# Sparse attention's scores from queries and keys split into a high and a low part

## What is computed

```python
q = _rope(q.reshape(B_, S_, G, Hg, Dh).transpose(0, 2, 3, 1, 4), pos)      # G=2 groups, Hg=4 heads, Dh=64
k_cmp = _rope(_compress(kv(kc), pe[0], w1[0], w2[0]), cmp_end)             # 31 compressed keys per group
s = jnp.einsum('bgjtd,bgcd->bgjtc', q, k_cmp) * scale                      # compressed scores
p_cmp = _masked_softmax(s, cmp_end[None, :] <= pos[:, None])
k_slc = _rope(kv(ks), pos)                                                 # keys of the selected blocks
sc = jnp.einsum('bgjqd,bgqnld->bgjqnl', qi, kg) * scale                    # their scores
# window branch: the same with kw, vw; the three outputs are mixed by gates
```

## Time and profile before

| | |
|---|---|
| median of 3 runs | 2645.97 us |
| lowest and highest | 2643.62 and 2646.96 us |
| the profiled execution's own time | 2646.77 us |
| its span in the profile | 2645.5 us |
| PE busy | 2613.4 us, 99% |
| DVE busy | 1563.1 us, 59% |
| ACT busy | 1037.1 us, 39% |
| mean granted clock of PE | 0.997 |

### The profile page before, as it was taken

One profiled execution on the slowest core, in us unless ns is written; L12 is line 12 of the kernel. 1 busy time (PEld: TensorE's weight loads), 2 busy tenths in 40 slices (PEclk: granted clock), 3 DMA queues, 4 the chain that ended last, 5 costly groups with the idle time before them and its releaser, 6 DMA issues.

```text
span 2645.5 us, 33775 instructions
## 1 busy us (share of the span) xinstructions
PE 2613.4 (99%) x13925; PEld 2149.9 (81%) x13925; DVE 1563.1 (59%) x2805; ACT 1037.1 (39%) x1809; POOL 15.0 (1%) x43
## 2 busy tenths in 40 slices
PE   7999999999999999999999999999999999999999
PEld 5788888898888897767888889888888766888888
DVE  7766554458666366777766637653356687633334
ACT  4652343444222245664322224222234665422223
POOL 1000000000000000000000000000000000000000
PEclk9999999999999999999999999999999999999999
DMA  8255433225555234311655424633333511233222
GB/s 260 80 175 171 131 116 112 80 84 199 195 191 175 88 113 130 110 33 49 209 200 191 163 84 156 209 125 96 96 96 110 155 33 33 85 106 96 96 92 68
DMA packets 298241, 330.14 MB, mean 125 GB/s; under 512 B 13410, under 2 KB 248678, under 8 KB 298088
## 3 DMA queue, kind: packets, MB, share of 16 engines
q1 hardware_dynamic: 297716, 327.44, 38.8%
q10 hardware_dynamic: 372, 0.55, 0.1%
HBM read 319.56 MB, written 2.10 MB: 122 GB/s over the span
## 4 chain that ended last, share of the span: by engine, by line
PE 93%; DVE 5%; ACT 1%; DMA 0%; SPq 0%; issue 0%; DVEq 0%
PE bank L543 27%; PE bank L545 27%; PE bank L544 27%; PE bank L597 2%; PE bank L2536 1%; PE bank L2563 1%; PE bank L2176 1%; DVE w_lo L511 1%; DVE E L2658 1%; PE bank L571 0%; DMA mw<-in_w_mod 0%; PE bank L573 0%; PE bank L572 0%; PE bank L900 0%; PE bank L2351 0%; PE bank L587 0%
## 5 line engine op out<-in xcount | busy, mean ns | idle before, releaser
L543 PE MATMUL bank<-h_lo,w_hi 128*128 128x512 f32 (+1 forms) x2496 | 936.1, 375 | 2.6 <-DVE h_lo L742 1.5
L545 PE MATMUL bank<-h_hi,w_lo 128*128 128x512 f32 (+1 forms) x2496 | 918.5, 368 | 0.0
L544 PE MATMUL bank<-h_hi,w_hi 128*128 128x512 f32 (+1 forms) x2496 | 917.3, 368 | 0.0
L511 DVE TENSOR_TENSOR w_lo<-raw,w_hi 128x1024 fp32r<-128x1024 f32 (+1 forms) x420 | 489.1, 1200 | 373.3 <-ACT w_hi L505 373.1
L505 ACT ACTIVATE w_hi<-raw 128x1024 fp32r<-128x1024 f32 (+1 forms) x420 | 420.1, 1036 | 349.7 <-PE bank L545 335.3
L543 PEld LDWEIGHTS bank<-h_lo,w_hi 128*128 128x128 f32 x2496 | 471.0, 189 | 88.2 <-issue 7.2
L544 PEld LDWEIGHTS bank<-h_hi,w_hi 128*128 128x128 f32 x2496 | 471.2, 189 | 78.6 <-issue 4.1
L545 PEld LDWEIGHTS bank<-h_hi,w_lo 128*128 128x128 f32 x2496 | 470.2, 188 | 78.7
L543 PE MATMUL bank<-a_lo,w_hi 128*128 128x512 f32 (+1 forms) x1056 | 388.6, 368 | 0.0
L545 PE MATMUL bank<-a_hi,w_lo 128*128 128x512 f32 (+1 forms) x1056 | 384.0, 364 | 0.0
L544 PE MATMUL bank<-a_hi,w_hi 128*128 128x512 f32 (+1 forms) x1056 | 383.9, 364 | 0.0
(11 more groups left out here) (344 smaller groups left out, 2291.3 us busy)
## 6 DMA issues: line engine op xcount, KB each, us to landing
swf<-in_w_ada SPq DMA_DIRECT2D x60, 1024.0 KB, 7.6
raw<-in_ffn_w_gate SPq DMA_DIRECT2D x44, 1024.0 KB, 5.3
raw<-in_ffn_w_up SPq DMA_DIRECT2D x44, 1024.0 KB, 5.3
raw<-in_w_in SPq DMA_DIRECT2D x40, 1024.0 KB, 5.2
raw<-in_ffn_w_down SPq DMA_DIRECT2D x32, 1024.0 KB, 5.3
raw<-in_w_in SPq DMA_DIRECT2D x32, 512.0 KB, 5.3
raw<-in_ffn_w_down SPq DMA_DIRECT2D x16, 768.0 KB, 4.4
mw<-in_w_mod SPq DMA_DIRECT2D x8, 1024.0 KB, 12.0
```

The lines of the kernel that those rows point to most:

```text
L511: nc.vector.tensor_tensor(o, r, half(w_his[place_of[i]], i, h)[0].bitcast(F32), ALU.subtract).then_inc(*w_lo.up((i, h)))
L543: nc.tensor.matmul(o, w1, al, start=start, stop=False)
L544: nc.tensor.matmul(o, w1, ah, start=False, stop=False)
L545: return nc.tensor.matmul(o, w2, ah, start=False, stop=stop)
```

## The change

Operands of the sparse scores are split into a high part (rounded to fp32r) and a low part (the rest).

- Queries: tile qa holds head 0's high part on the lower 64 partitions and its low part on the upper 64; tile qb holds head 1's low part below and its high part above. Keys: ksh and kwh hold the high parts on all 128 rows, once per half; kl the low parts.
- A score step becomes two fp32r products on 128 rows (high over low queries, with high keys), then two fp32r products on 64 rows (high queries with low keys), accumulated in the same banks. Low times low is left out.
- The compressed scores become, for each of 4 pairs c and 2 heads, one product with kc_hi (32 columns) and one with kc_lo (32 columns): 16 per call instead of 4 in fp32.
- For p = 4 to 9 ACT writes the high part in two copies of 64 x 512 (act_high) and DVE the low part in two subtractions of 64 x 512 (dve_low_part). DVE's sum of the rotary embedding now stays in its temporary tile, and ("rd", l, p) is now the low part's.
- The compressed keys get one sum on DVE, one copy on ACT (act_kc_high), two subtractions on DVE (dve_kc_low), which stand behind dve_w(("vv", l), 2).
- sp_cross copies high parts (waiting for ACT) and then waits for tile 9's low part; sp_cross_low copies the low parts, waiting for the last value product of the differential attention.
- The third output's copies move from step 28 to 32 (OC_STEP), since its place in a_hi now holds low keys until the last score.

```diff
+    def act_high(l, p):
+        act.wait_ge(dve, ("rx", l, p))
+        for par in range(2):
+            nc.scalar.activation(high_of(p, par), pair(p)[1][par * 64:par * 64 + 64, :], ACT.Copy).then_inc(
+                *act.up(("rh", l, p) if par else ("rh", l, p, 0)))
+
+    def dve_low_part(l, p):
+        dve.wait_ge(act, ("rh", l, p))
+        for par in range(2):
+            r = slice(par * 64, par * 64 + 64)
+            if p < 8:
+                o = qab[par][64 - par * 64:128 - par * 64, (p - 4) * 512:(p - 4) * 512 + 512]
+            else:
+                o = kl[p - 8][0][r, :]
+            nc.vector.tensor_tensor(o, pair(p)[1][r, :], high_of(p, par).bitcast(F32), ALU.subtract).then_inc(
+                *dve.up(("rd", l, p) if par else ("rd", l, p, 0)))
...
@@ def dve_kc
-        dve.wait_ge(pool, ("zn", l))
-        for par in range(2):
-            r = slice(par * 64, par * 64 + 64)
-            nc.vector.tensor_tensor(kcz[r, par * 64:par * 64 + 64], lamt[r, 64:128], lamt[r, 128:192], ALU.add).then_inc(
-                *dve.up(("kc", l, par)))
+        nc.vector.tensor_tensor(kb, kb, kc, ALU.add).then_inc(*dve.up(("kc", l, 0)))
+
+    def act_kc_high(l):
+        act.wait_ge(dve, ("kc", l, 0))
+        nc.scalar.activation(kc_hi, lamt[:, 64:128], ACT.Copy).then_inc(*act.up(("kch", l)))
+
+    def dve_kc_low(l):
+        dve.wait_ge(act, ("kch", l))
+        dve.wait_ge(pool, ("zn", l))
+        for par in range(2):
+            r = slice(par * 64, par * 64 + 64)
+            nc.vector.tensor_tensor(kc_lo[r, par * 64:par * 64 + 64], lamt[r, 64:128], kc_hi[r, :].bitcast(F32),
+                                    ALU.subtract).then_inc(*dve.up(("kc", l, 1 + par)))
@@ def pe_cs
-        pe.wait_ge(dve, ("kc", l, 1))
+        pe.wait_ge(dve, ("kc", l, 2))
         for c in range(4):
-            kz = kcz[:, :].rearrange("p (a g c) -> p a g c", a=2, g=2)[:, :, c // 2, :]
-            m = nc.tensor.matmul(t[:, c * 64:c * 64 + 64].rearrange("p (a c) -> p a c", a=2),
-                                 nq[:, c * 512 + b * 128:c * 512 + b * 128 + 128], kz, start=True, stop=True)
+            g = c // 2 * 32
+            for par in range(2):
+                o = t[:, c * 64 + par * 32:c * 64 + par * 32 + 32]
+                q = qab[par][:, c * 512 + b * 128:c * 512 + b * 128 + 128]
+                nc.tensor.matmul(o, q, kc_hi[:, g:g + 32], start=True, stop=False)
+                m = nc.tensor.matmul(o, q, kc_lo[:, par * 64 + g:par * 64 + g + 32], start=False, stop=True)
@@ def scores
+            pe.wait_ge(cross_low_in[br], l)
             t = [bank(("ns", l, s, par), N_SC) for par in range(2)]
+            q = [qab[par][:, c * 512 + b * 128:c * 512 + b * 128 + 128] for par in range(2)]
+            for par in range(2):
+                nc.tensor.matmul(t[par][:, 0:w], q[par], kh[br][:, g * 512:g * 512 + w], start=True, stop=False)
             for par in range(2):
                 r = slice(par * 64, par * 64 + 64)
-                k0 = (g ^ par) * 512
-                nc.tensor.matmul(t[par][:, 0:w], nq[r, c * 512 + b * 128:c * 512 + b * 128 + 128],
-                                 (ks, kw)[br][r, k0:k0 + w], start=True, stop=True).then_inc(
-                                     *pe.up(("ns", l, s, par)))
+                nc.tensor.matmul(t[par][:, 0:w], q[par][r, :], kl[br][g ^ par][r, 0:w], start=False, stop=True).then_inc(
+                    *pe.up(("ns", l, s, par)))
@@ def act_mixer
         for i in range(2):
             steps(1)
+            if i:
+                act_high(l, 5)
             act_rope(l, ("nq", l, i, 0), 4 + 2 * i)
             steps(1)
             act_w(("nq", l, i), 2)
             steps(1)
             act_rope(l, ("nq", l, i, 1), 5 + 2 * i)
-            steps(2)
+            steps(2 if i else 1)
+            act_high(l, 4 + 2 * i)
+            steps(0 if i else 1)
         act_hidden(l, 0)
         steps(1)
+        act_high(l, 7)
         act_rope(l, ("kk", l, 0), 8)
         act_hidden_silu(l, 0)
         steps(1)
         act_w(("kk", l), 2)
         steps(1)
         act_rope(l, ("kk", l, 1), 9)
-        steps(4)
+        steps(2)
+        act_high(l, 8)
+        steps(1)
+        act_high(l, 9)
+        steps(1)
         act_hidden_turn(l, 0)
         steps(2)
         act_kc(l)
         steps(2)
+        act_kc_high(l)
         act_w(("vv", l), 2)
@@ def dve_mixer
         dve_rope(l, 5)
-        steps(3)
+        dve_low_part(l, 4)
+        steps(1)
+        dve_low_part(l, 5)
+        steps(2)
...
         dve_rope(l, 7)
+        dve_low_part(l, 6)
         dve_hidden(l, 0)
         gx1 = dve_gx(l, 1)
         for i in range(3):
             steps(1)
+            if i == 0:
+                dve_low_part(l, 7)
             next(gx1)
...
         dve_rope(l, 9)
-        steps(5)
+        dve_low_part(l, 8)
+        steps(1)
+        dve_low_part(l, 9)
+        steps(4)
         dve_vv(l)
         dve_kc(l)
         dve_w(("vv", l), 2)
+        dve_kc_low(l)
         steps(1)
         dve_cm(l, 0)
@@ def sp_cross
-        for n, kd in enumerate((ks, kw)):
-            sp.wait_ge(dve, ("rd", l, 8 + n))
+        for n in range(2):
+            sp.wait_ge(act, ("rh", l, 8 + n))
...
+        sp.wait_ge(dve, ("rd", l, 9))
+
+    def sp_cross_low(l):
+        sp.wait_ge(pe, ("dav", l, 15))
```

More of the change, by code:

```diff
@@ L333, in carve, with here @@
         place = [start]
-        def here(name, cols):
-            t = sb(name, cols, at=place[0])
+        def here(name, cols, dt=F32):
+            t = sb(name, cols, dt, at=place[0])
             place[0] += (cols * 4 + 63) // 64 * 64
@@ L378, in build @@
     w_los.append(sb("w_lo2", 2048, F32R, at=phase0 + 4352 + 1024 + 2048 + 4096 + 8192))
-    nq = here("nq", 2048)
-    ks, kw = here("ks", 1024), here("kw", 1024)
+    kh = [sb(n, 1024, F32R, at=phase0 + 4352 + 1024 + 2048 + 4096 + 8192 + 4096 * i) for i, n in enumerate(("ksh", "kwh"))]
+    qab = [sb("qa", 2048, F32R, at=phase0 + 4352 + 1024 + 2048 + 4096)]
+    here("qk", 4096)
     at_swf = phase0 + 4352 + 1024 + 2048 + 4096 + 16384
     vsw = here("vsw", 1024)
-    kcz = here("kcz", 128)
+    kc_hi, kc_lo = [here(n, c, F32R)[:, :] for n, c in (("kc_hi", 64), ("kc_lo", 128))]
     VB = here("VB", 512)
@@ L390, in build @@
     tmp += [here(f"tmp{i}", 512) for i in (5, 6)]
+    qab.append(here("qb", 2048, F32R))
+    kl = [[sb(f"kl{i}{j}", 512, F32R, at=o) for j, o in enumerate(at)]
+          for i, at in enumerate(((at_flip, phase0 + 4352 + 1024 + 2048), (at_a + 12288, phase0 + 4352 + 1024 + 2048 + 2048)))]
     exs = [sb(f"ex{i}", 512, at=at_a + 16384 * i + 14336) for i in range(2)]
@@ L2106, in build @@
     cross_in = [sig(f"cross{i}_in") for i in range(2)]
+    cross_low_in = [sig(f"cross_low{i}_in") for i in range(2)]
     PAIR = {("dq", 0): 0, ("dq", 1): 1, ("dk", 0): 2, ("dk", 1): 3, ("n0", 0): 4, ("n0", 1): 5, ("n1", 0): 6,
@@ L2124, in rope_where, with high_of @@
             d = [(every, dk[:, (p - 2) * 512:(p - 2) * 512 + 512])]
-        elif p < 8:
-            d = [(every, nq[:, (p - 4) * 512:(p - 4) * 512 + 512])]
         else:
-            d = [(every, (ks, kw)[p - 8][:, 0:512])]
+            d = [(every, pair(p)[1][:, :])]
         return t, d
+    def high_of(p, par):
+        r = slice(par * 64, par * 64 + 64)
+        if p < 8:
+            return qab[par][r, (p - 4) * 512:(p - 4) * 512 + 512]
+        return kh[p - 8][r, par * 512:par * 512 + 512]
+    def act_high(l, p):
[7 more added lines that the diff above has]
+            r = slice(par * 64, par * 64 + 64)
+            if p < 8:
+                o = qab[par][64 - par * 64:128 - par * 64, (p - 4) * 512:(p - 4) * 512 + 512]
[3 more added lines that the diff above has]
+                *dve.up(("rd", l, p) if par else ("rd", l, p, 0)))
     def act_rope(l, key, p):
@@ L3093, in pool_mixer @@
             pool.wait_ge(dve, acc_key(b4, -1))
-        nc.gpsimd.memset(kcz[:, :], 0.0).then_inc(*pool.up(("zn", l)))
+        nc.gpsimd.memset(kc_lo.bitcast(F32), 0.0).then_inc(*pool.up(("zn", l)))
         pool.wait_ge(ld_ws, l)
@@ L3101, in sp_cross @@
     def sp_cross(l):
-        for n, kd in enumerate((ks, kw)):
-            sp.wait_ge(dve, ("rd", l, 8 + n))
+        for n in range(2):
+            sp.wait_ge(act, ("rh", l, 8 + n))
+            for par in range(2):
+                r, o = slice(64 - par * 64, 128 - par * 64), slice(par * 64, par * 64 + 64)
+                nc.sync.dma_start(kh[n][r, par * 512:par * 512 + 512].bitcast(F32),
+                                  kh[n][o, par * 512:par * 512 + 512].bitcast(F32)).then_inc(
+                    *cross_in[n].up(l, 16))
+        sp.wait_ge(dve, ("rd", l, 9))
+    def sp_cross_low(l):
+        sp.wait_ge(pe, ("dav", l, 15))
+        for n in range(2):
             for par in range(2):
                 r, o = slice(par * 64, par * 64 + 64), slice(64 - par * 64, 128 - par * 64)
-                nc.sync.dma_start(kd[r, 512:1024], kd[o, 0:512]).then_inc(*cross_in[n].up(l, 16))
```

(1 more changed line is left out.)

12 lines of the change are left out of this document (7 added, 5 removed).

## The result

With the change the kernel takes 2679.86 us (median of 4 runs, 2678.92 to 2680.82); the kernel before, run beside it, 2645.65 (4 runs, 2643.62 to 2646.96). The ratio is 1.0132, with a 95% interval of 1.0119 to 1.0144. So the change costs 34.2 us, where 22.6 were forecast (2668.6, range 2648 to 2679): slower, as forecast, but by half as much again, and just past the end of the range. The profiled execution took 2680.82 us with a span of 2679.5.

What follows compares the result with a forecast made beforehand. TensorE was taken to bound the kernel, with DVE leading where sparse scores begin. Per mixer 2.7 + 4.1 + 1.3 + 3.6 + 0.9 - 1.3 = 11.3 us, 22.6 for both, gave 2668.6 us, range 2648 to 2679.

Steps and rivals of the forecast that it cites:

- tiles 4 and 5: Their ACT copies and DVE subtractions cost nothing, falling into DVE's waits for PE; tightest release 0.1 us before PE asks.
- A: Operand work of tiles 6 and 7 makes attention steps 10 and 11 late and delays PE: 2.7 us per mixer.
- B: Operand work of tiles 8 and 9 delays PE around attention steps 15 to 17: 4.1 us, 3.5 in one pause.
- C: Compressed keys' low part queues behind vv's weight subtractions; PE waits 2.5 us; with the doubled products 3.6 + 0.9 us.
- score steps: fp32r passes in sparse score steps 10 to 31 save PE 1.3 us per mixer; steps 0 to 9 give nothing.
- I count one such fall behind it: One fall of PE's clock to 0.50 behind B's pause, 1.3 us per mixer.
- so all terms count twice: The second sparse mixer is the same as the first 1016.4 us later, so 11.3 us per mixer becomes 22.6.
- Rival (1): A and B hide because half-height operations take half the time or ACT reaches them earlier: 2652.4 us, chance 0.17.
- signs: What would show the forecast; for score steps, durations of 0.9, 0.7, 0.55 and 0.5 us.
- rival (4): fp32r at these shapes issues in two passes like fp32, 47 us over 44 score steps: about 2716 us, chance 0.02.
- Rival (2): Faster: score-step moves cost nothing, A and B hide, the present clock fall goes: 2641.0, reaching 2635 us; chance 0.11.
- Rival (3): The 64-row fp32r pair isn't concurrent and the 128-wide pass is dear: 2678.6 us, chance 0.15.

Runs made afterwards that it cites:

- e_nocl: e_abc with the products of the compressed keys' low part left out, 8 products per block instead of 16: 2641.25 us.
- e_fill: The changed kernel with filler products, whose results nobody reads, put into PE's pauses, every wait kept: 2670.77 us.
- e_abc: The changed kernel with the added ACT and DVE operand work at A, B, C and tile 5 reordered, same instructions otherwise: 2647.29 us.
- e_nopair: e_abc with the pair of 64-row products of each score step left out: 2624.47 us.
- e_128: e_abc with low keys laid on both partition halves, so each score step's second pair has 128 rows; nothing left out: 2637.12 us.
- e_wide: e_abc with each product of the compressed keys' high part streaming its 32 columns eight times over: 2645.81 us.

## Why the prediction was wrong in its size

Per mixer, forecast and measured; the measured ones are from the shift of PE's starts against before, the compressed products' from e_nocl (as worked out there), and the clock's lower value from e_fill (9.1 / 2):

| | forecast | measured |
|---|---|---|
| tiles 4 and 5 | 0 | 0.56 |
| A | 2.7 | 3.4 |
| B without the clock | 4.1 | 4.8 |
| C, wait | 2.5 | 2.3 |
| C, compressed products | 2.0 | about 2.1 |
| score steps | -1.3 | -1.9 |
| clock | 1.3 | 4.5 to 5.6 |
| sum | 11.3 | 15.8 to 16.9 |
| shift of PE, mean of both mixers | | 16.9 |

The clock's upper value is what the other terms leave. It fits the step from e_abc to after: 32.6 us, of which the waits (0.56 + 3.4 + 4.8 + 2.3, twice) are 22.1 and 10.5 are left, 5.3 per mixer, and e_abc has one slow stretch more per mixer than before, the cheap one behind block 2. The lower value is short because e_fill has one more than before in mixer 1, and its products take a little time. The 1.1 us between the two were not measured by themselves.

**The step that failed: "I count one such fall behind it".** The forecast knew that a pause draws a slow stretch, had a row that priced it, and applied it to one pause only, the longest. Others drew theirs too: the 1.0 us at A with what followed it, the 2.2 at C, and one of the four blocks of narrow products. This is 3.2 to 4.3 of the 5.6 us that are missing per mixer. That each of the three places was worth 10 to 12 us in all, while their waits are 4.0, 4.8 and 2.2 us per mixer, says the same from the other side: waits and the clock share the gain.

Not every pause drew one. Of the mixers with the pause, outside e_fill, B's was followed by a slow stretch in 6 of 6, C's in 6 of 6 (in four of them a double one), and A's in 4 of 6. With this "so all terms count twice" failed as well: the waits are the same in both mixers, but the slow stretches are not the same in place, length or price, and mixer 2 lost 3.8 us more than mixer 1. What decides whether a pause of A's size draws one stays open.

**Tiles 4 and 5, costed at nothing.** Step 7's two banks come late by DVE's subtraction of tile 5; L2202 there lasts 1.20 instead of 0.63 us. The walk had found 0.1 us to spare, and that is less than its own error: the operations on 64 partitions were taken at 1.15 to 1.25 us a pair on ACT and 1.22 on DVE. The groups of instructions of after show, without any discount for half the partitions (minimum, median and maximum in ns):

```profile
L2144 ACT ACTIVATE qb<-tmp x8: 626/629/631, 1031.2 to 2094.1; 64x512 fp32r<-64x512 f32 x8
L2155 DVE TENSOR_TENSOR qb<-tmp,qb x8: 686/687/689, 1035.8 to 2095.4; 64x512 fp32r<-64x512 f32 x8
```

and a pair takes 1.26 and 1.41 us. Rival (1)'s premise, half the time for half the height, is thereby out. This is also most of what A and B are over: 0.7 us at either, two pairs on each engine in the chain.

**A and B, right in place and kind.** The pause of 3.5 us at B is 3.49, ended by the ACT copy that was named, with the two idle times of ACT and DVE behind it. The rest of B is a wait of L602 for DVE, 1.40 us where the forecast had 0.6 outside its pause. A has its two late steps: laid beside before, whose mixer starts 1.5 us later, PE's shift goes from -0.95 at step 10 to 0.07 at step 11, 2.13 at step 12 and 2.46 at step 13.

**C, right.** 2.5 us were forecast for kc_lo, 2.23 measured; 16 products at 0.11 us, 1.81 in all against 1.75.

**Score steps.** The gain per step is 0.16, 0.13, 0.09 and 0.00 us where 0.17, 0.13, 0.09 and -0.11 were forecast: the second 128-wide product starts 0.06 us behind the first instead of 0.11. (The steps' own durations are up to 0.1 above those listed as signs; part of the gain lies in the entry, 0.24 instead of 0.31 us.) The move was costed at 0.2 us and kept; it is 0.30 with a pair, by e_nopair and e_128. Two of the forecast's products are a little off and change nothing: rival (4)'s 47 us are 44 by its own terms, and 6 x 3 x 0.1 is 1.8. Rival (2), moves that cost nothing, is out in the change, but e_128 shows that its gain is there to be had by having no move: about 5 us per mixer, the slow stretches that went with them not counted. Rival (3) named nearly the time that was measured, 2678.6, by a mechanism that did not happen: the 64-row products start together. A forecast can meet the number and be wrong.
I had set 0.11 us for narrow products by a row. The Trainium skill (TensorE: Matmul & The Clock Gate, section LDWEIGHTS (loading the stationary operand)) gives a formula by which a weight load of 128 columns takes an estimated 107 ns, and the trace's 0.11 us agrees with it.

## What to carry to other kernels

A new operation on an engine that feeds the critical one costs by where it stands in the hop between engines: the same 16 us of ACT and DVE per mixer made the kernel 32.6 us longer in one order than in another. For each new pause of TensorE, not the longest alone, allow for a stretch at half the clock behind it (1.3 us here where TensorE leads), and take as the range that it comes or does not: of the pauses here some drew one in every mixer and others only in some. Then ask who leads in that stretch; where another engine does, it costs less or nothing. And compare two variants by their numbers of such stretches before you lay a difference of a few microseconds to an edit. Products on fewer rows that start together pay only if the move to them and back (0.30 us here) is less than the columns they save.

## What the runs showed of the hardware that was not expected

- A step with two products on 64 rows between 128-row ones costs 0.30 us more than its columns, at every width (0.52, 0.46, 0.40, 0.35 us with 0.21, 0.16, 0.11, 0.05 of columns, an estimate from the width at 2.4 GHz). No weight load runs ahead there (0.33 us from the last 128-row product to load and product, in e_abc).
- A second 128-wide product behind one of the same width starts 0.06 us after it; the third and fourth start 0.10 and 0.12 us apart.
- Behind 16 products of 32 columns, PE busy throughout, the granted clock went to 0.51 in e_abc; over all kernels with such products it did so behind block 2 in 6 mixers of 16.
- One stretch of 3.4 us at 1.2 GHz cost 1.25 to 1.43 us where PE leads (e_nocl, e_128, e_wide), 0.5 where DVE leads (e_fill), and nothing inside place A (mixer 1 of after).
- ACT and DVE take as long for 64 x 512 as for 128 x 512 (0.63 and 0.69 us against 0.63 and 0.69 in the earlier trace rows).
